# Stick-breaking attention stage of a decoder step: score pairs and turned chunks alternate, the scan's second operand lies in PSUM, VectorE copies every second head's turned chunks

## The reference, cut to what matters

```
def stick_breaking_attend(q, q_pos, k, v, k_pos):
    z = jnp.einsum('bqhd,blhd->bhql', q, k).astype(jnp.float32) * (HEAD_DIM ** -0.5)
    strict = (k_pos[None, :] < q_pos[:, None])[None, None]
    log_keep = jnp.where(strict, jax.nn.log_sigmoid(-z), 0.0)
    after = lax.cumsum(log_keep, axis=3, reverse=True) - log_keep
    log_a = jnp.where(strict, jax.nn.log_sigmoid(z) + after, -jnp.inf)
    return jnp.einsum('bhql,blhd->bqhd', jnp.exp(log_a).astype(v.dtype), v)
```

## Time and profile before

| what | us |
|---|---|
| median of 3 runs (2389.12 to 2395.8) | 2395.78 |
| the profiled execution, its own time | 2393.49 |
| its span, first to last instruction | 2391.5 |
| busy in the span: PE, DVE, ACT, POOL | 2142.7, 1444.0, 766.1, 182.6 |
| the stage of the change, first scan to last copy of o | 193.4 |

### The profile page before, as it was taken

How to read it: one execution, slowest core, us unless ns; L and a number is a source line. 1 busy time by engine, 2 the same in 40 slices (tenths; PEclk the granted TensorE clock), 3 DMA queues, 4 the chain that set the end, 5 groups by cost and what they waited for, 6 DMA issues and landing times. The chain is left out here.

```text
span 2391.5 us, 36882 instructions
## 1 busy us (share of the span) xinstructions
PE 2142.7 (90%) x13337; PEld 1775.6 (74%) x13337; DVE 1444.0 (60%) x2439; ACT 766.1 (32%) x1421; POOL 182.6 (8%) x120
## 2 busy tenths in 40 slices
PE   4876999999997887887876989899999999999995
PEld 4833888888885555555554878689999999999994
DVE  4448967664587776654443543336656656666566
ACT  4046011111216776664433432222122122122122
POOL 0000000000007884001000000000000000000000
PEclk7988999999999898998998999999999999999997
DMA  4321222232223101540899532021011111111102
GB/s 152 100 50 53 88 84 84 84 119 83 84 69 91 40 29 47 168 163 22 313 356 330 180 116 95 0 75 53 26 53 50 29 53 37 41 53 33 46 21 88
DMA packets 186052, 218.73 MB, mean 91 GB/s; under 512 B 28828, under 2 KB 119324, under 8 KB 184796
## 3 DMA queue, kind: packets, MB, share of 16 engines
q1 hardware_dynamic: 185300, 217.20, 27.7%
q10 hardware_dynamic: 648, 0.15, 0.0%
HBM read 181.17 MB, written 36.13 MB: 91 GB/s over the span
## 5 line engine op out<-in xcount | busy, mean ns | idle before, releaser
L2434 DVE TENSOR_TENSOR x_all<-x_all,ff_down 128x512 f32<-128x512 f32 x396 | 269.9, 688 | 159.3 <-PE ff_down L2338 159.1
L2323 PE MATMUL ff_up<-m_hi,ff_up_hi 128*128 128x368 f32 x1056 | 348.2, 330 | 8.1 <-DVE ff_up_lo L2411 8.1
L2324 PE MATMUL ff_up<-m_lo,ff_up_hi 128*128 128x368 f32 x1056 | 349.0, 331 | 0.0
L2325 PE MATMUL ff_up<-m_hi,ff_up_lo 128*128 128x368 f32 x1056 | 347.3, 329 | 0.0
L419 PE MATMUL pr_acc<-pr_w_hi,h_hi 128*128 128x512 f32 x720 | 281.0, 390 | 16.3 <-DVE pr_w_lo L356 16.3
L420 PE MATMUL pr_acc<-pr_w_lo,h_hi 128*128 128x512 f32 x720 | 280.7, 390 | 0.0
L421 PE MATMUL pr_acc<-pr_w_hi,h_lo 128*128 128x512 f32 x720 | 280.6, 390 | 0.0
L819 DVE TENSOR_SCALAR_CACHE_REDUCE bi_flags<-scores,bi_thr 128x384 bf16<-128x384 f32 (+6 forms) x231 | 215.9, 992 | 1.2
L2323 PEld LDWEIGHTS ff_up<-m_hi,ff_up_hi 128*128 128x128 f32 x1056 | 198.8, 188 | 9.3 <-DVE ff_up_lo L2411 8.5
L2324 PEld LDWEIGHTS ff_up<-m_lo,ff_up_hi 128*128 128x128 f32 x1056 | 198.7, 188 | 0.8
L2325 PEld LDWEIGHTS ff_up<-m_hi,ff_up_lo 128*128 128x128 f32 x1056 | 198.8, 188 | 0.0
(11 more groups left out here) (273 smaller groups left out, 3572.6 us busy)
## 6 DMA issues: line engine op xcount, KB each, us to landing
out_proj<-pr_staged SPq DMA_DIRECT2D x90, 256.0 KB, 2.0
up_raw<-in_w_up SPq DMA_DIRECT2D x44, 512.0 KB, 4.9
w_raw<-in_w_in SPq DMA_DIRECT2D x10, 2048.0 KB, 8.1
sa_keys<-in_cache_k_a SPq DMA_DIRECT2D x64, 256.0 KB, 4.5
sa_values<-in_cache_v_a SPq DMA_DIRECT2D x64, 256.0 KB, 7.6
sa_keys<-in_cache_k_b SPq DMA_DIRECT2D x64, 256.0 KB, 6.5
sa_values<-in_cache_v_b SPq DMA_DIRECT2D x64, 256.0 KB, 5.5
ff_down_raw<-in_w_down SPq DMA_DIRECT2D x22, 512.0 KB, 3.5
```

The lines of the kernel that those rows point to most:

```text
L2323: pe.matmul(up[n][:], w, hi[:, c, at], start=c == 0, stop=False)
L2324: pe.matmul(up[n][:], w, lo[:, c, at], start=False, stop=False)
L2325: ins = pe.matmul(up[n][:], w_rest, hi[:, c, at], start=False, stop=c == KC - 1)
L2434: dve.tensor_tensor(at, at, down[n][:], ALU.add).then_inc(down_added.sem, 1)
```

## The change

- The scan's second operand becomes `unread`, one column in a PSUM bank of its own that DVE fills with 1.0 once, read for every column of the scan. The result is the same, as the operand isn't used.
- To free that bank, o has one bank in place of two: `use` of the first tile of a group waits until the group before is evacuated (o_out at b in place of b - 1).
- The turned chunks of head 1 are copied to `prob_t` by DVE, those of head 0 by ACT as before; `turns_out` becomes two semaphores, one for each head.
- DVE's step n becomes: evacuation, copies of head 1's chunks of tile n-3, scans of tile n.
- `woven` (new) deals the turned chunks of tile n-3 out between the score pairs of tile n. PE's step n becomes: first score pair, use(n-4), its share of chunks, second pair, its share, and so on, then q and k of the next pair. ACT's step alternates the sigmoids of a pair with head 0's chunks in the same way.

The diff, cut to its core:

```
+    place_of = [sum(d[1] == TURNS[c][1] for d in TURNS[:c]) for c in range(len(TURNS))]
+    turns_before = [sum(d[0] < g and d[1] == 0 for d in TURNS) for g in range(NG + 1)]
...
-    o = [ctx.enter_context(nc.psum_tensor(f"st_o{b}", [P, 4 * P], F32)) for b in range(2)]
+    o = ctx.enter_context(nc.psum_tensor("st_o", [P, 4 * P], F32))
+    unread = ctx.enter_context(nc.psum_tensor("st_unread", [P, 1], F32))
...
+    def woven(n):
+        beside = turns_of[n - TURN_LAG] if TURN_LAG <= n < NG + TURN_LAG else []
+        if n >= NG:
+            return [(None, beside)]
+        parts, m = len(scores_of[n]) // 2, len(beside)
+        return [(k, beside[k * m // parts:(k + 1) * m // parts]) for k in range(parts)]
...
             def use(g):
...
-                pe.wait_ge(turns_out, turns_of[g][-1] + 1)
+                for hh in range(2):
+                    pe.wait_ge(turns_out[hh], turns_before[g + 1])
...
-                if t == first and b >= 2:
-                    pe.wait_ge(o_out, b - 1)
+                if t == first and b >= 1:
+                    pe.wait_ge(o_out, b)
...
             for n in range(NG + USE_LAG):
+                for k, chunks_beside in woven(n):
+                    if k is not None:
+                        score(n, k)
+                    if not k and n >= USE_LAG:
+                        use(n - USE_LAG)
+                    for c in chunks_beside:
+                        turn(c)
                 if n < NG:
-                    score(n)
                     i, t = divmod(n, NT)
                     for b in QK_WITH.get(t, ()) if i + 1 < PAIRS else ():
                         turn_qk(i + 1, b)
-                if n >= USE_LAG:
-                    use(n - USE_LAG)
-                if TURN_LAG <= n < NG + TURN_LAG:
-                    turn(n - TURN_LAG)
...
+            def take_turns(g):
+                r = tile_rows(g % NT)
+                if g >= 2:
+                    dve.wait_ge(used, g - 1)
+                for c in turns_of[g]:
+                    hh, k0, n = TURNS[c][1:]
+                    if hh == 1:
+                        w = tile_rows(k0)
+                        dve.wait_ge(turns, c + 1)
+                        dve.tensor_copy(prob_t[g % 2][1][0:w, k0:k0 + n, 0:r],
+                                        turned[c % NTB][0:w, 0:n, 0:r]).then_inc(turns_out[1], 1)
+
+            dve.memset(unread[:], 1.0).then_inc(unread_set, 1)
+            dve.wait_ge(unread_set, 1)
             for n in range(NG + USE_LAG + 1):
+                if n >= USE_LAG + 1:
+                    i, t = divmod(n - USE_LAG - 1, NT)
+                    if t + 1 == O_GROUPS[group_of[t]][1]:
+                        evacuate(i, group_of[t])
+                if TURN_LAG <= n < NG + TURN_LAG:
+                    take_turns(n - TURN_LAG)
                 if n < NG:
...
-                        dve.tensor_tensor_scan(x[:, ::-1], x[:, ::-1], x[:, ::-1], 1.0, ALU.mult,
-                                               ALU.bypass).then_inc(scanned, 1)
-                if n >= USE_LAG + 1:
-                    i, t = divmod(n - USE_LAG - 1, NT)
-                    if t + 1 == O_GROUPS[group_of[t]][1]:
-                        evacuate(i, group_of[t])
+                        dve.tensor_tensor_scan(x[:, ::-1], x[:, ::-1], unread[0:r, :].to_broadcast([r, w]), 1.0,
+                                               ALU.mult, ALU.bypass).then_inc(scanned, 1)
```

More of the change, by code:

```diff
@@ L1019, in stick @@
     turned = [ctx.enter_context(nc.psum_tensor(f"st_turned{b}", [P, 4, P], F32)) for b in range(NTB)]
-    o = [ctx.enter_context(nc.psum_tensor(f"st_o{b}", [P, 4 * P], F32)) for b in range(2)]
+    o = ctx.enter_context(nc.psum_tensor("st_o", [P, 4 * P], F32))
+    unread = ctx.enter_context(nc.psum_tensor("st_unread", [P, 1], F32))
+    unread_set = sem("unread_set")
     mask_made, mask_stored = sem("mask_made"), sem("mask_stored")
@@ L1023, in stick @@
     stored = [sem(f"stored{b}") for b in range(2)]
-    made, taken, scanned, weighed, turns, turns_out, used, o_out = (
-        sem(x) for x in ("made", "taken", "scanned", "weighed", "turns", "turns_out", "used", "o_out"))
+    made, taken, scanned, weighed, turns, used, o_out = (
+        sem(x) for x in ("made", "taken", "scanned", "weighed", "turns", "used", "o_out"))
+    turns_out = [sem(f"turns_out{hh}") for hh in range(2)]
     tiled = proj.rearrange("(t p) n -> p t n", p=P)
@@ L1086, in turn_qk, with score @@
                 ins.then_inc(made, 1)
-            def score(g):
+            def score(g, k):
                 i, t = divmod(g, NT)
                 r = tile_rows(t)
-                if t == 0:
+                if t == 0 and k == 0:
                     pe.wait_ge(taken, copies_of[i, len(QK) - 1] + 1)
                 last = scores_of[g][-2][0]
-                for c, hh, a, w in scores_of[g]:
+                for c, hh, a, w in scores_of[g][2 * k:2 * k + 2]:
                     if hh == 0:
@@ L1100, in score @@
                         ins.then_inc(made, 1)
-                for c, hh, a, w in scores_of[g][-2:]:
+                for c, hh, a, w in scores_of[g][2 * k:2 * k + 2] if 2 * k + 2 == len(scores_of[g]) else ():
                     at = slice(t * P - a, t * P - a + r)
@@ L1104, in score, with turn @@
                               skip_group_check=True).then_inc(made, 1)
-            def turn(g):
+            def turn(c):
+                g, hh, k0, n = TURNS[c]
                 r = tile_rows(g % NT)
[L1108 to L1118, removed]
+                pe.wait_ge(weighed, 2 * g + hh + 1)
+                if c >= NTB:
+                    pe.wait_ge(turns_out[TURNS[c - NTB][1]], place_of[c - NTB] + 1)
+                for j in range(n):
+                    kt = k0 + j
+                    w = tile_rows(kt)
+                    ins = pe.transpose(turned[c % NTB][0:w, j, 0:r], prob[g % R][hh][0:r, kt * P:kt * P + w],
+                                       ident[0:r, 0:r])
+                ins.then_inc(turns, 1)
             def use(g):
@@ L1133, in use @@
                     for hh in range(2):
-                        ins = pe.matmul(o[b % 2][half(hh), at:at + r], v_rows[i % 2][0:w, kt, half(hh)],
+                        ins = pe.matmul(o[half(hh), at:at + r], v_rows[i % 2][0:w, kt, half(hh)],
                                         prob_t[g % 2][hh][0:w, kt, 0:r], start=kt == 0, stop=kt == t,
@@ L1167, in take_qk, with open_tile @@
                 ins.then_inc(taken, 1)
-            def open_tile(g):
+            def open_tile(g, k):
                 r = tile_rows(g % NT)
-                if g >= R:
+                if g >= R and k == 0:
                     act.wait_ge(weighed, 2 * (g - R + 1))
                     act.wait_ge(turns, turns_of[g - R][-1] + 1)
-                for c, hh, a, w in scores_of[g]:
+                for c, hh, a, w in scores_of[g][2 * k:2 * k + 2]:
                     act.wait_ge(made, c + 1)
@@ L1177, in open_tile, with take_turn @@
                     act.activation(prob[g % R][hh][0:r, a:a + w], banks[c % NS][0:r, 0:w], ACT.Sigmoid).then_inc(taken, 1)
-            def take_turns(g):
-                r = tile_rows(g % NT)
-                if g >= 2:
+            def take_turn(c):
+                g, hh, k0, n = TURNS[c]
+                r, w = tile_rows(g % NT), tile_rows(k0)
+                if g >= 2 and c == turns_of[g][0]:
                     act.wait_ge(used, g - 1)
[L1183 to L1188, removed]
+                act.wait_ge(turns, c + 1)
+                act.activation(prob_t[g % 2][hh][0:w, k0:k0 + n, 0:r], turned[c % NTB][0:w, 0:n, 0:r],
+                               ACT.Copy).then_inc(turns_out[0], 1)
             for b in range(len(QK)):
@@ L1192, in _ @@
             for n in range(NG + TURN_LAG):
+                for k, chunks_beside in woven(n):
+                    if k is not None:
+                        open_tile(n, k)
+                    for c in chunks_beside:
+                        if TURNS[c][1] == 0:
+                            take_turn(c)
                 if n < NG:
-                    open_tile(n)
                     i, t = divmod(n, NT)
@@ L1197, in _ @@
                         take_qk(i + 1, b)
-                if n >= TURN_LAG:
-                    take_turns(n - TURN_LAG)
         @block.vector
@@ L1204, in evacuate @@
                 first, last = O_GROUPS[k]
-                b = i * len(O_GROUPS) + k
                 dve.wait_ge(used, i * NT + last)
@@ L1209, in evacuate @@
                 w = min(last * P, NP_ROWS) - first * P
-                dve.tensor_copy(o_all[i % 2][:, first * P:first * P + w], o[b % 2][:, 0:w]).then_inc(o_out, 1)
-            for n in range(NG + USE_LAG + 1):
+                dve.tensor_copy(o_all[i % 2][:, first * P:first * P + w], o[:, 0:w]).then_inc(o_out, 1)
+            def take_turns(g):
[11 more added lines that the diff above has]
+            dve.wait_ge(unread_set, 1)
+            for n in range(NG + USE_LAG + 1):
```

(2 more changed lines are left out.)

## The result

The changed kernel takes **2419.74 us** (median of 4 runs, 2418.66 to 2423.7), the kernel before 2394.7 beside it: ratio 1.0113, interval 1.0096 to 1.013, slower by 25 us. The profiled execution took 2418.8 us, its span 2416.8 (before 2391.5).

A forecast was written before the change was run, and what follows sets the result against it. Scan and POOL product alternating bound wide tiles, PE and ACT narrow ones. First pair -5.0, later pairs 3 x 1.2, tail +4.0, clock +10.5: +13.1 on 2393.49, 2406.6; plus 2.3 for the median, 2409; range 2384 to 2426.

The forecast's parts named there:

- full-clock links: Steps of a head pair, each between the ends (S) of two tiles' scans, at PE's full clock: 49.4 us in sum.
- S8 to S0: From the end of tile 8's scans to that of the next tile 0's: copies 1.2, scans 0.7, in sum 2.0 us.
- S6 to S7: From the end of tile 6's scans to that of tile 7's: 1.2 of waiting for PE, 0.8, 4.4: 6.4 us.
- the clock's price in S2 to S6: PE at half clock after tile 8's small blocks: 1.3, 0.9 and 1.3 us more in three steps, 3.5 a pair.
- part 3's: One bank for o: before the first use of tiles 4 to 7, PE idles 3 to 4 us for o's evacuation.
- S7 to S8: From the end of tile 7's scans to that of tile 8's: 11.5 us, of which DVE stands for 5.3.
- The fall in step 8: PE's clock may fall after standing 3.6 us for o: 2.8 us more, 11 over four pairs, 2420; outside the forecast.
- The first pair: First head pair, with nothing of an earlier pair to turn or use: 35.0 us against 40.0, 5.0 less.
- The tail: After the last tile 8's scans, use and turning no longer beside scans: 12.6 us against 8.7, 4.0 more.
- part 4: Alternation in tiles 4 to 8: some 0.2 us a step for PE, covered by other waits; without them 1 us a pair.
- The waits hide: Rival: PE and DVE stay out of each other's way, each step costs its longest engine; 2363 to below 2385; chance 0.20.
- The scan is held: Rival: POOL's products still hold the scan despite its PSUM operand; 7 us more a pair, some 2430; chance 0.05.

The follow-up runs named there:

- parts 1 and 3 together: Of the change, only the PSUM scan operand and one bank for o, evacuated behind the scans, q and k turned later; against the kernel before: 2392.27 us, 0.999.

## Why the prediction was right, and where not

**Right: the direction and its reason.** The scan alone costs 2.09 ns a column with an operand in PSUM too (2267 ns, my 2.27 us), and DVE's sum of 33.1 us a pair came out at 32.7. The full-clock links held: S8 to S0 1.99 (2.0), S0 to S1 5.87 (5.8), S1 to S2 4.88 (4.8), S6 to S7 6.65 (6.4). So did the clock's price in S2 to S6: 1.4, 1.0 and 1.6 us beyond the full-clock links (6.21 against 4.8, 6.31 against 5.3, 10.44 against 8.8), where I had 1.3, 0.9 and 1.3. The standing that I called part 3's (3 to 4 us) is 3.31, and with the clock kept up S7 to S8 takes the 11.5 us of the chain (11.7).

**Too small: the sum, +13.1 where +25 was measured.** Three terms:
- *The fall in step 8*, which I left out of the forecast though PE's standing of 3.6 us stood in the text. It comes in every pair: S7 to S8 12.8 to 13.4 instead of 11.5, four times 1.5 us. The run with PE kept busy gives 1.3 of it back in that step. My price for it, 2.8, was twice too high, since only use and the first chunk are slow; the second score pair takes 1.13 us, as the first does ahead of the standing.
- *The first pair*: -1.0 instead of -5.0. Beside step 8, S6 to S7 took 6.67 us, as in the later pairs, where I had 5.2, and S3 to S5 8.3, not 7.0.
- *The tail*: +6.7 instead of +4.0: the clock's mean there is 0.78, and 0.50 over its last 3 us.

These make 11 of the 12 us that were missing. The forecast of 2409 thus lay 10.7 us low. The time came out where I had put the fall alone, at 2420, but by the three terms together, which is luck.

**Wrong: the price of part 4 by itself.** I put alternation at 0.2 us a step, covered by other waits. Undone, it gives 13 or 14 us. The links of step 8 were right, but I booked them under part 3 alone: it is alternation that puts the second score pair behind the use that waits for o, and without alternation or copies on DVE parts 1 and 3 together cost nothing (2392.3), with no standing for o in step 8.

**The rivals.** *The waits hide* named the point that decides, o_out before PE needs it, and the moved evacuation makes it so. But it reached 2388, not 2363 to 2385: I let tiles 0 to 3 cost 16 us a pair (PE) and 4 to 8 22.7 (DVE). The kernel with the evacuation alone moved, its second pair cut at S3:

```profile
767.59:786.75 19.16, 17.65 (x171) 11.94 (x170) 9.78 (x18) 8.45 (x22) 6.77 (x8) 0.86 0.12 35
786.75:815.30 28.55, 25.73 (x199) 16.30 (x200) 22.97 (x18) 22.96 (x60) 16.41 (x11) 0.92 0.22 59
```

DVE's work in tiles 4 to 8 is 23.0 us as I had it, but PE is busy for 25.7 there, and the stretch takes 28.5: PE, not DVE, is the busiest engine in both. *The scan is held* I priced at 7 us a pair; it is 3.5, and 6.8 in the first. The Trainium skill (SBUF — State Buffer, who interferes with whom) has a VectorE instruction with at most one SBUF input, outside the two-port modes, free of GpSimd; the 2267 and 1996 ns agree. The larger fixed term for a PSUM source that the Trainium skill gives (VectorE: DVE Perf Modes, section on the TRN2 errata; 120 cycles against 58) doesn't show in the scan: 1024 columns take 2267 ns, and the scans alone had put it at 2280 (2297 less 8 columns). My copy of 16 columns could not tell, as no copy from SBUF stood beside it.

## What to carry to other kernels

Before freeing a busy engine, ask what the others have left to do in the time it gives back: here DVE was freed of 13 us a pair and POOL of 17, the wide tiles got 3 us shorter, and PE's work lengthened the narrow ones by as much. In an in-order queue the place of a short instruction can be worth more than the speed of the long ones: three copies a pair of under 0.7 us each, moved ahead of two scans, were worth 31 us. But ask what stands behind it: with nothing there that the other engines need soon, the same move was worth 2. Where a buffer is given up, look first at what its release is queued behind.

## What was not expected of the hardware

PE's standing of 3.31 us in step 8, and of 2.73 us in the kernel with the one bank alone, were each followed by use of tile 4 at 2.40 us instead of 1.31; 2.42 us at 902 us of the kernel before was not followed by a fall. Nor does it take a standing of that length. In the kernel with the evacuation alone moved PE stands for 1.04 us at most at a time between 795 and 812 us, and the clock falls all the same: it is 0.50 from 812.1 to 815.4, and use of tile 5 takes 2.62 us instead of 1.53:

```profile
811.81 2.62 PE L1147 MATMUL st_o<-st_prob_t,st_v_rows 128*64 128x128 f32 x24
```

So the length of one standing doesn't say whether the clock falls, and what does is not shown by these runs.
